# Products of the identity with itself, put into TensorE's instruction stream at six places of a two-layer diffusion block on one core

## The reference, cut to what matters

```python
def trunk_layer(x, cond, lp, ctx_k=None, ctx_v=None):
    mod = jax.nn.silu(cond) @ lp['w_ada'] + lp['b_ada']
    sh1, sc1, g1, sh2, sc2, g2 = jnp.split(mod[:, None, :], 6, axis=-1)
    h = x * (1.0 + sc1) + sh1
    q, k, v, z_hy, gate_a, gate_b = jnp.split(h @ lp['w_in'], SPLITS, axis=-1)
    attn = ...                      # windowed attention with sinks
    hy = hyena_branch(z_hy, lp)     # x0 * (long convolution by FFT of x1 * u)
    merged = jax.nn.sigmoid(gate_a) * (attn @ lp['w_pa']) + jax.nn.sigmoid(gate_b) * (hy @ lp['w_pb'])
    x = layer_norm(ALPHA * x + g1 * (merged @ lp['w_out']), lp['ln1_g'], lp['ln1_b'])
    ffn = conv_ffn(x * (1.0 + sc2) + sh2, lp)
    x = layer_norm(ALPHA * x + g2 * ffn, lp['ln2_g'], lp['ln2_b'])
    return x, k, v
```

## Time and profile before

| | us |
|---|---|
| median of 3 runs | 2191.92 |
| lowest and highest | 2183.78, 2192.34 |
| profiled execution | 2190.16 |
| its span, first to last instruction | 2188.3 |
| mean granted clock over the span | 0.975 |
| TensorE busy, of the span | 2063.0 (94%) |
| DVE, ACT, POOL busy | 1163.6, 761.7, 161.5 |

### The profile page before, as it was taken

How to read it: one execution, slowest core, us unless ns; L and a number is a source line. 1 busy time by engine, 2 the same in 40 slices (tenths; PEclk the granted TensorE clock), 3 DMA queues, 4 the chain that set the end, 5 groups by cost and what they waited for, 6 DMA issues and landing times.

```text
span 2188.3 us, 30546 instructions
## 1 busy us (share of the span) xinstructions
PE 2063.0 (94%) x13110; PEld 1947.3 (89%) x13110; DVE 1163.6 (53%) x1699; ACT 761.7 (35%) x1118; POOL 161.5 (7%) x180
## 2 busy tenths in 40 slices
PE   4989998899999999999998999799999999999997
PEld 2468888799998999999998888689999999999996
DVE  5523456775746677777644545772335533234435
ACT  2253344532226331133225344452224533123323
POOL 0020000000015000000023000010003300000011
PEclk8999999999999999999999999899999999999999
DMA  5423112144421334533321110221221121222121
GB/s 227 160 90 109 39 37 87 49 140 140 154 97 59 135 142 144 206 141 135 137 83 68 61 37 20 106 68 58 87 78 66 70 78 54 92 78 78 60 67 48
DMA packets 33871, 207.07 MB, mean 95 GB/s; under 512 B 4054, under 2 KB 4615, under 8 KB 15048
## 3 DMA queue, kind: packets, MB, share of 16 engines
q1 hardware_dynamic: 29320, 185.02, 23.8%
q10 hardware_dynamic: 3120, 11.99, 1.4%
q0 software_dynamic: 1296, 8.11, 1.0%
HBM read 196.98 MB, written 8.13 MB: 94 GB/s over the span
## 4 chain that ended last, share of the span: by engine, by line
PE 86%; DVE 6%; ACT 5%; issue 2%; DMA 1%; POOL 0%; SPq 0%; ACTq 0%; DVEq 0%; POOLq 0%
PE gemm_psum L574 50%; PE gemm_psum L604 14%; PE gemm_psum L624 3%; PE gemm_psum L587 3%; PE aux_psum L689 3%; PE gemm_psum L642 3%; PE aux_psum L674 2%; PE aux_psum L741 2%; PE gemm_psum L514 2%; PE gemm_psum L729 1%; PE gemm_psum L467 1%; ACT h_src_rows L1080 1%; PE aux_psum L698 1%; PE aux_psum L498 1%; ACT w_hi L1028 1%
## 5 line engine op out<-in xcount | busy, mean ns | idle before, releaser
L574 PE MATMUL gemm_psum<-h_hi,w_hi 128*128 128x322 f32 x2176 | 505.9, 314 | 9.4 <-DVE gates L1763 3.9
L574 PE MATMUL gemm_psum<-h_hi,w_lo 128*128 128x322 f32 x2176 | 502.4, 312 | 0.0
L574 PE MATMUL gemm_psum<-h_lo,w_hi 128*128 128x322 f32 x2176 | 501.3, 312 | 0.0
L1456 DVE TENSOR_TENSOR w_lo<-w_raw,w_hi 128x2048 fp32r<-128x2048 f32 (+2 forms) x144 | 287.7, 1998 | 306.7 <-ACT w_hi L1028 305.0
L574 PEld LDWEIGHTS gemm_psum<-h_hi,w_hi 128*128 128x128 f32 x2176 | 369.6, 190 | 15.1 <-issue 10.6
L574 PEld LDWEIGHTS gemm_psum<-h_lo,w_hi 128*128 128x128 f32 x2176 | 369.6, 190 | 0.0
L574 PEld LDWEIGHTS gemm_psum<-h_hi,w_lo 128*128 128x128 f32 x2176 | 369.1, 190 | 0.0
L1028 ACT ACTIVATE w_hi<-w_raw 128x2048 fp32r<-128x2048 f32 (+2 forms) x144 | 239.5, 1663 | 170.4 <-PE gemm_psum L604 65.6
L1444 DVE CUSTOM_DVE_ANT_0 aux_psum<-w_raw,cond_by_row 128x1024 f32<-128x1024 f32 x160 | 191.0, 1256 | 4.2 <-DMA w_raw<-in_ada_t 4.0
L1573 DVE SCALAR_TENSOR_TENSOR x<-gemm_psum,mod,x 128x128 f32<-128x128 f32 (+2 forms) x144 | 55.3, 434 | 164.8 <-PE gemm_psum L604 131.4
L604 PE MATMUL gemm_psum<-act_hi,w_lo 128*128 128x322 f32 x616 | 141.9, 311 | 0.0
(11 more groups left out here) (298 smaller groups left out, 3249.5 us busy)
## 6 DMA issues: line engine op xcount, KB each, us to landing
w_raw<-in_w_up SPq DMA_DIRECT2D x44, 1024.0 KB, 4.8
w_raw<-in_ada_t SPq DMA_DIRECT2D x40, 1024.0 KB, 4.8
w_raw<-in_w_down SPq DMA_DIRECT2D x32, 704.0 KB, 4.1
w_raw<-in_w_gate SPq DMA_DIRECT2D x16, 1024.0 KB, 4.8
w_raw<-in_w_z SPq DMA_DIRECT2D x12, 1024.0 KB, 4.7
w_raw<-in_ada SPq DMA_DIRECT2D x8, 1024.0 KB, 4.9
w_raw<-in_w_proj SPq DMA_DIRECT2D x16, 512.0 KB, 3.3
w_raw<-in_w_out SPq DMA_DIRECT2D x8, 1024.0 KB, 4.7
```

The lines of the kernel that those rows point to most:

```text
L574: last = mm(gp[:, 2 * (t % 2) + hf, 0:HALF], w[:, off + P * kk:off + P * (kk + 1)], moving(kk, lo)[:, hf * HALF:(hf + 1) * HALF], start=kk ...
L1456: TT(wlo[s][:, 0:n], raw[STEP[(lane.layer, "g", g)] % 2][:, 0:n], f32(whi[s][:, 0:n]), ALU.subtract).then_inc(sem["w_split"], raised("w_sp ...
```

## The change

A helper issues n products in plain f32 of the 128 x 128 identity with itself, without any wait of its own, into a PSUM range whose content nobody reads afterwards. It is called at six places of TensorE's program: ahead of the q product of layer 1 (16); in both layers after the transposes of Hyena (12), ahead of the wait for the first inverse (26) and ahead of the up product (8); in layer 1 ahead of the second gate product (14); and ahead of the final transposes (24). That is 16 + 2·(12 + 26 + 8) + 14 + 24 = 146 products, or 292 records. Nothing else is changed.

```diff
+        def keep_clock(n, to):
+
+            for _ in range(n):
+                mm(to, ident[:, :], ident[:, :], start=True, stop=True)
+
         def ln_stats(w, h, at):
...
+            if L:
+                keep_clock(16, ax[:, 3, 0:P])
             opening(0, "qkv_mm", lambda c, p_, hf: gp[:, 2 * c + p_, 0:HALF], q_free, 0, q_between)
...
             u_transposed(4)
+            keep_clock(12, ax[:, 2, 0:P])
...
                 spectrum(p_, U_V[p_])
 
+            keep_clock(26, ax[:, 2, 0:P])
             pe.wait_ge(sem["y_ready"], due("y_ready", 2))
...
             for m in range(KD):
                 g = at_g("gate", m)
+                if m == 1 and L:
+                    keep_clock(14, ax[:, 0, 0:P])
                 h_gemm(g, 2, "gate_mm", m == 0)
...
             for hf in range(2):
                 if hf == 0:
+                    keep_clock(8, ax[:, 3, 0:P])
                     opening(at_g("up", 0), "up_mm",
...
         for b in range(NB):
+            if b == 0:
+                keep_clock(24, gp[:, 2, 0:P])
             pe.wait_ge(sem["x_norm"], KD if b < 2 else 2 * KD)
```

## The result

| | before | after |
|---|---|---|
| median, us | 2190.57 (20 runs) | 2195.33 (20 runs) |
| lowest and highest | 2183.53, 2196.41 | 2188.00, 2202.89 |
| profiled execution | 2190.16 | 2188.00 |
| its span | 2188.3 | 2186.0 |
| mean granted clock over the span | 0.975 | 0.986 |

The ratio of the changed kernel to the one before is 1.0028, 95% interval [1.0016, 1.0041]: 6.1 us slower, 3.5 to 9.0. That is within the 0.5% that I called "no change", and the time is inside the range. But the forecast was +1.25 us, and this is more. Note the trap in the table: the profiled execution of the changed kernel is the fastest of its 20, 2.2 us *shorter* than that of before. Taken alone, these two traces say that the change is a gain. One run of the kernel before beside Experiment 2, 2469.62 us at a mean clock of 0.776, is a slow one and is left out of all comparisons.

A forecast was written before the change was run, and what follows sets the result against it. TensorE holds 86% of the chain, its clock halved in short stretches mostly behind waits. +3.1 - 0.3 - 1.15 - 0.4 = +1.25 us on the profiled 2190.16 gives 2191.4, stated as 2191.5 us; range 2184 to 2198.

The forecast's parts named there:

- The price of a product: Any identity product on TensorE: two records in plain f32, 0.22 us, with 0.21 and 0.28 as ends.
- gate: Layer 1's second gate, 14 products with no wait to lie in, nothing gives the delay back: +3.1 us (2.9 to 3.9).
- Rival (c): All calls: a product costs twice as much, 0.44 us, so 25 us more, 2215 us; chance 0.04.
- Behind the transposes: Hyena, 12 products in a 3.43 us wait: spectra start at full clock, DVE's idle time won, -0.3 and -1.15 us.
- (d): Attention: its falls of the clock move between runs, widening the range by 2 to 3 us each way; no chance given.
- Ahead of the inverse: Hyena, 26 products: context's inverse in time by 0.3 us, clock falls again near inverse(1); -0.4 us both layers (-3.8 to +1.5).
- Up product, q and end: The 8, 16 and 24 products: gains run into waits for other engines, 0 each; end -1.65 to +0.9.
- rival (a): Clock holds at inverse(1) and the end: 1.55 + 2.25 + 1.65 = 5.45 us instead of 0.4, 2186.3 us; chance 0.18.
- Rival (b): All calls: the products don't count for the clock, only the gate's 3.1 us remain, 2193.3 us; chance 0.13.

The follow-up runs named there:

- Experiment 2: Four kernels against the one before: 56 products at the gate alone 1.0058; calls moved into TensorE's longest waits 0.9994; Hyena's calls with 52 1.0018; the change again 1.0021.
- kernels with attention calls: Kernel before plus five products per attention block, in the wait for the first p_t, in both layers: 0.9970; in layer 1 alone: 0.9981; some also carry the change's calls.
- norms_end: Changed kernel with only the 16 ahead of q of layer 1, the 8 ahead of both up products and the 24 at the end; 1.0001 to the kernel before.
- before_2: The kernel before, unchanged, traced a second time for its stages; attention of layer 1 took 135.79 us.
- behind: Changed kernel without the gate's 14; the 26 moved behind the context's inverse, 36 instead of 24 behind the first 16 final transposes; 0.9994 to the kernel before.
- the sharpest timing: The change added to the kernel before with attention products in layer 1 alone: 1.0000 against 0.9981 without the change, 3.9 +- 1.0 us above it.
- the plain ones: The changed kernel against the kernel before, without attention products, timed twice: 1.0028 (6.1 us) and 1.0021 (4.6 us).
- the steady pair: Kernel before with five products per attention block in layer 1 alone, without and with the change: 0.9981 and 1.0000 to the kernel before.
- the two timings: The changed kernel against the kernel before, first timing 1.0028, and once more on the same chip as other kernels 1.0021.
- the long execution: Profiled execution of the changed kernel's second timing (1.0021), nothing else changed: span 2198.6 us, with 23.9 us at half clock in layer 1's attention.
- no_gate: Changed kernel without the 14 products ahead of layer 1's second gate product; 1.0001 to the kernel before, highest of 12 runs 2193.65 us.

## Why the prediction was wrong, point by point

Three steps of the prediction failed. It took the 1.15 us in front of the first product by the filter in layer 1 as won (0.36 by the mean of the traces), from one execution. It counted one gain for the inverses of both layers, where layer 0 lost. And it took the attention's falls as 2 to 3 us to each side, where they are up to 13.5. With every term as measured the sum by stages is +2.4 us and not +1.25; the rest up to the measured 3.9 to 6.1 is open. The forecast was also set low: the sum was added to one execution, 1.8 us below the median of the three. Added to that median (2191.92) it is 2193.2, and 2191.5 lies below the kernel before.

Stage lengths from the traces, in us. "Without" are kernels whose trace has no call in that stage, "with" those that have the change's own; means, with the number of traces:

| stage, call | without | with | difference | forecast |
|---|---|---|---|---|
| gates of layer 1 (14) | 174.40 (12) | 177.35 (7) | +2.95 | +3.1 |
| spectra of layer 0 (12) | 21.38 (9) | 21.00 (8) | -0.38 | -0.3 |
| spectra of layer 1 (12) | 21.36 (9) | 21.00 (8) | -0.36 | -1.15 |
| inverses of layer 0 (26) | 35.97 (6) | 36.44 (6) | +0.47 | -0.4 for both layers |
| gates of layer 0 (none; behind the inverses) | 180.64 (6) | 180.39 (6) | -0.25 | 0 |
| inverses of layer 1 (26) | 36.83 (9) | 36.43 (8) | -0.40 | as above |
| from layer 0's out product to layer 1's q (8) | 547.1 (12) | 547.1 (8) | 0 | 0 |
| from q of layer 1 to its attention (16) | 88.6 (12) | 88.6 (8) | 0 | 0 |
| end of layer 1 (8 and 24) | 568.1 (11) | 568.4 (7) | +0.3 | 0 |

For the inverses and the gates of layer 0 the kernels with attention calls in that layer are left out, since these change them. The differences add up to +2.4 us, against +1.25 in the prediction.

**The price of a product** was right: 0.223 us for a forecast of 0.22. So was the **gate**, the one call on the path. Rival (c) is out: 0.112 us a record at full clock.

**Behind the transposes** failed, in layer 1. The mechanism was right (the clock holds, DVE's idle time ahead of the first product by the filter is gone), the term was mis-sized: 1.15 us forecast, 0.36 measured. It was read from one execution, and that was the dearest of nine. The chain of waits tells why. In the trace of before it goes through twelve products at half clock; these are that trace, `norms_end`, whose trace too has a fall there, and `before_2`, another execution of the very kernel before, with its clock at that place:

```profile
1387.68 5.47 PE gemm_psum L729 x12
```

```profile
1386.63 4.61 PE gemm_psum L729 x12
```

```profile
1393.82 1.28 DVE v_lo L1460 x2
1395.11 0.69 DVE prod L1702
```

```profile
1389.50:1392.90 3.40, 2.77 (x7) 2.22 (x8) 3.16 (x6) 2.64 (x6) 0.00 (x0) 0.50 1.00 424
```

In the trace of before the twelve took 5.47 us and the spectra 22.26. In `norms_end` the clock was at half for less of them: 4.61 and 21.40. In `before_2` the spectra began at half clock too (at 1390.13), but the full clock was back at 1392.9, after six products, and the chain goes over DVE's own work, not over TensorE: 21.12 us, 0.1 from what the 12 products reach. So whether the stretch at half clock that I priced lies on the path depends on how long it lasts, which differs from one execution to the next. The prediction knew that the attention's falls move (d), and did not apply it to the stretches that it meant to win.

**Ahead of the inverse**: right that the context's inverse is in time (2.87 us of wait left), right that the clock falls again. Wrong by the sign in layer 0 (+0.47 in its own stage, +0.2 with the gates behind it), within the ends that were given (-3.8 to +1.5): in two of the six traces with the calls the fall lasted longer (36.88 and 37.09 us against 36.1 to 36.2), as in layer 1 of the trace of before. In these two traces the gates of layer 0 are 1.0 and 1.1 us shorter than in the other four, so there the longer fall cost next to nothing in the end.

**Up product, q and end**: 0 as said, but for the end's +0.3, which is no more than that stage scatters (567.3 to 568.7 us in the eleven traces without calls). The 1.65 us in rival (a) for the last transposes don't exist: `behind` has them at full clock and ends no earlier. The wait for `w_split` in q of layer 1 grew to 1.88 us, from the 0.64 of the earlier trace rows, which is where that call's time went.

**Rival (d)** was the other mis-sized term: "2 to 3 us each way", and it is 13.5 us between the best and the worst trace in layer 1's attention alone, and single runs of the changed kernel lie as far apart (2188 to 2203). The median of three runs and one trace are no base for a sum of 1 us. **Rival (b)** gave a time near the result (2193.3), for a wrong reason: the products do count for the clock, in Hyena, in the attention and with `behind` in the inverse. What fits is the rest of its arithmetic: the gate's 3.1 us remain, and what the other calls win doesn't matter much.

**What stays open.** The stages sum to +2.4 us; the sharpest timing says 3.9 +- 1.0, the plain ones 4.6 and 6.1. Between half and two and a half microseconds are in no stage that I could name. What the plain kernels lie above the steady pair may be the attention of layer 1 falling more often with the change in. The traces don't decide it (130.76, 130.76 and 141.00 us in its three). The single runs hint at it: 12 of the 32 changed runs in the two timings lie above 2199.5 us, and of the 54 runs of before beside them 6 lie above 2195.6, the same less 3.9. Such a run was traced once, the long execution (2200.69 us, clock 0.978, attention 141.00). Against it stands `no_gate`, which has every call that comes ahead of that attention and none such among its 12 runs. So it isn't shown.

## What to carry to other kernels

A product that keeps the clock is free only inside a wait, and worth something only where the engine itself holds the chain behind that wait: here that was the attention, whose waits of 1.2 to 1.5 us looked too short to matter and were worth some 6.6 us, and not the longest waits, behind which another engine or the stores were due anyway. Ten calls of five products there gave 0.9970, and with Hyena's twelve and twenty-six beside them 0.9957.

When runs of one kernel lie 10 us apart, find the stage that scatters before pricing anything of 1 us, by a second trace of the same kernel. Once that stage is held steady, small parts can be timed that drown otherwise.

## What the hardware showed that I had not expected

The same program, with the same wait of 1.19 us for `p_t`, kept the full clock in one execution and lost it for 23.9 us in another, and nothing in the program tells the two apart. The Trainium skill, TensorE: Matmul & The Clock Gate, Part 1, says of a kernel's start that the number of slow matmuls differs from run to run; here the same holds in the middle of a program, and is worth 13 us there. After the fall the clock stayed at half over a block of small matmuls in which TensorE was busy without a break by the trace (23.90 of 23.90 us). The half clock stretched small and large products alike, to nearly twice their time. A head's transposes and P·V came every 1.28 us at full clock and every 2.45 at half; a pair of records of 322 columns every 0.30 and every 0.54 (trace of before, from 457.63 on). The lengths printed for such a pair, 0.46 and 0.74 us, differ by less, since by the trace each pair ends after the next has begun: go by the distance of the starts.
